# A recurrence on TensorE: four filling products between weighted values and turned scores are taken out, three put in front of state steps, one behind the turns

## The reference, cut to what matters

```python
def rwkv7_mixer(p, mu, w0, w2, a0, a2, g2, k_k, k_a, r_k, lnx_w, lnx_b):
    ...
    def step(S, inp):
        r_t, k_t, v_t, w_t, kk_t, a_t = inp
        sa = jnp.einsum('bhvk,bhk->bhv', S, -kk_t)
        S = (S * w_t[:, :, None, :]
             + sa[..., None] * (kk_t * a_t)[:, :, None, :]
             + v_t[..., None] * k_t[:, :, None, :])
        y = jnp.einsum('bhvk,bhk->bhv', S, r_t)
        return S, y

def first_block(...):
    hn = rms_norm(h, norm_mix_pre[l])
    p = hn @ w_in[l]
    p_rw, p_ret, g_rw, g_ret = _split(p, IN_SIZES)
    y_rw = rwkv7_mixer(p_rw, ...)
```

## Time and profile before

| | |
|---|---|
| median of three executions | 2320.08 us |
| the profiled execution's own time | 2319.33 us |
| its span, first to last instruction | 2317.5 us |
| granted TensorE clock, mean | 0.999 |
| TensorE busy | 2281.6 us (98%), 12764 matmuls |
| VectorE / ScalarE / GpSimd busy | 1380.8 / 752.1 / 914.4 us |
| chain that ended last | TensorE 88%, VectorE 6%, ScalarE 2% |

### The profile page before, as it was taken

The page is one execution under the profiler, slowest core; times in us unless marked ns, Lnnn a source line. Parts: engine busy times, 40 slices in busy tenths (PEclk is TensorE's granted clock), DMA queues, the critical chain, the costliest instruction groups (busy, mean ns, idle before and its releaser), DMA issues.

```text
span 2317.5 us, 33458 instructions
## 1 busy us (share of the span) xinstructions
PE 2281.6 (98%) x12764; PEld 1882.9 (81%) x12764; DVE 1380.8 (60%) x1615; ACT 752.1 (32%) x1243; POOL 914.4 (39%) x538
## 2 busy tenths in 40 slices
PE   7999999999999999999999999999999999999998
PEld 6788888888888888888888887888888887777776
DVE  7755374537543754576628796555551487756775
ACT  4311131113111211334325334444432445114442
POOL 3311231123112313413366457777744445422164
PEclk9999999999999999999999999999999999999999
DMA  3211211121111113573544432222156433211123
GB/s 148 81 55 46 74 55 55 55 72 47 64 55 65 64 46 115 196 236 133 191 140 146 165 107 82 82 82 82 64 198 210 145 122 100 67 59 40 34 82 119
DMA packets 71317, 230.65 MB, mean 100 GB/s; under 512 B 6800, under 2 KB 11024, under 8 KB 70672
## 3 DMA queue, kind: packets, MB, share of 16 engines
q1 hardware_dynamic: 40560, 138.76, 18.8%
q10 hardware_dynamic: 30624, 89.97, 10.6%
HBM read 182.04 MB, written 46.66 MB: 99 GB/s over the span
## 4 chain that ended last, share of the span: by engine, by line
PE 88%; DVE 6%; ACT 2%; issue 1%; DVEq 1%; POOL 1%; DMA 1%; POOLq 0%; ACTq 0%; SPq 0%
PE psg L774 7%; PE psg L779 7%; PE psg L781 6%; PE psg L640 4%; PE psg L645 4%; PE psg L644 4%; PE psa L1246 3%; PE psa L1248 2%; PE psa L1249 2%; PE psb L1246 2%; PE psb L1248 2%; PE psb L1249 2%; PE psa L874 2%; PE psb L861 1%; PE psg L742 1%; PE psg L1458 1%
## 5 line engine op out<-in xcount | busy, mean ns | idle before, releaser
L527 POOL CAST whi<-wraw 128x1024 fp32r<-128x1024 f32 (+1 forms) x144 | 167.0, 1159 | 1102.4 <-PE psg L774 512.0
L529 POOL TENSOR_TENSOR wlo<-wraw,whi 128x1024 fp32r<-128x1024 f32 (+1 forms) x144 | 367.8, 2554 | 20.8 <-issue 0.2
L774 PE MATMUL psg<-xhi,whi 128*128 128x512 f32 x640 | 259.2, 405 | 0.0
L781 PE MATMUL psg<-xhi,wlo 128*128 128x512 f32 x640 | 258.0, 403 | 0.0
L779 PE MATMUL psg<-xlo,whi 128*128 128x512 f32 x640 | 256.2, 400 | 0.0
L640 PE MATMUL psg<-xhi,whi 128*128 128x512 f32 x496 | 195.7, 394 | 2.7 <-issue 2.1
L645 PE MATMUL psg<-xhi,wlo 128*128 128x512 f32 x496 | 194.8, 393 | 0.0
L644 PE MATMUL psg<-xlo,whi 128*128 128x512 f32 x496 | 193.9, 391 | 0.0
L604 POOL TENSOR_TENSOR wlo<-wraw,whi 128x1024 fp32r<-128x1024 f32 (+1 forms) x50 | 112.1, 2243 | 139.8 <-ACT whi L2783 74.3
L774 PEld LDWEIGHTS psg<-xhi,whi 128*128 128x128 f32 x640 | 120.9, 189 | 25.8 <-issue 6.3
L781 PEld LDWEIGHTS psg<-xhi,wlo 128*128 128x128 f32 x640 | 120.8, 189 | 20.9 <-issue 1.0
(11 more groups left out here) (699 smaller groups left out, 5873.9 us busy)
## 6 DMA issues: line engine op xcount, KB each, us to landing
wraw<-w SPq DMA_DIRECT2D x208, 512.0 KB, 3.5
later_scratch<-stage ACTq DMA_DIRECT2D x40, 512.0 KB, 2.6
sraw<-w SPq DMA_DIRECT2D x16, 512.0 KB, 3.9
ff_scratch<-ring ACTq DMA_DIRECT2D x10, 512.0 KB, 2.6
ff_scratch<-ff ACTq DMA_DIRECT2D x10, 512.0 KB, 2.6
ff<-ff_scratch ACTq DMA_DIRECT2D x5, 1024.0 KB, 7.6
RV<-later_scratch SPq DMA_DIRECT2D x4, 1024.0 KB, 11.9
RG<-later_scratch SPq DMA_DIRECT2D x4, 1024.0 KB, 5.6
```

The lines of the kernel that those rows point to most:

```text
L527: pool.tensor_copy(whi[:, u, 0:width], wraw[:, u, 0:width])
L529: pool.tensor_tensor(wlo[:, u, 0:width], wraw[:, u, 0:width], whi[:, u, 0:width].bitcast(F32), ALU.subtract).then_inc(w_ready, 1)
L774: mm = pe.matmul(ps[:, cols], whi[:, slot, w_cols], xhi[:, k, cols], start=(k == 0), stop=False)
L781: mm = pe.matmul(ps[:, cols], wlo[:, slot, w_cols], xhi[:, k, cols], start=False, stop=(k == KT - 1))
```

## The change

In each of the 16 groups, the four fillings between L842 and L849 go. The fillings behind L849 become six instead of five. Three single fillings are put in: behind outputs(1) and so in front of step(0,1), behind additions(1,0) in front of step(1,0), behind additions(1,1) in front of step(1,1). The sum over a group stays 87.

```diff
                     mm.then_inc(sem("dv_full"), 1)
-                    fill(4)
 
                     pe.wait_ge(sem("at_unit"), 4 * i + g + 1)
                     for q in range(4):
                         mm = pe.transpose(bank[2][:, q * P:q * P + P], SC[:, q, 0:P], m(M_ID))
                     mm.then_inc(sem("x_full"), 1)
-                    fill(5)
+                    fill(6)
...
                     state_step(0, 0)
                     outputs(1)
+                    fill(1)
                     state_step(0, 1)
                     additions(1, 0)
+                    fill(1)
                     state_step(1, 0)
                     additions(1, 1)
+                    fill(1)
                     state_step(1, 1)
                 fill(16)
```

## The result

The changed kernel takes 2332.24 us (median of six executions, 2331.0 to 2332.74) against 2319.31 us for the kernel before in the same comparison: ratio 1.0055, 95% interval 1.0045 to 1.0065, or 12.9 us more. It was forecast to be slower, at 2329.9 us within 2324.0 to 2333.5, so direction and range hold. The sum gave 9.8 us more than before, 3 us too few.

The account below looks back on a forecast made before the run. TensorE, busy 98% of the span, was taken as the bound. Sixteen groups at -0.92 + 0.23 + 1.28 = +0.59 give +9.4, with 0.4 for M +9.8 us: forecast 2329.9 us, range 2324 to 2333.5.

Parts of the forecast that it names:

- Removed fillings: Four fillings between L842 and the turned scores L849 go: gain 0.92 us a group.
- The sixth filling: One more filling behind the turned scores L849, same shape on both sides: adds 0.23 us a group.
- Three fillings in the state part: Each makes two array-shape changes of one: 0.42 for each of two, 0.44 for the third, 1.28 us a group.
- A group +0.59: Sum for one group: -0.92 + 0.23 + 1.28 us; sixteen groups +9.4 us.
- this reading: The 0.15 us gap before L933 is the price of changing the array part in use, not a wait.
- M late in a pair's second group: L861's weight load waits for VectorE's M: 0.1 us in four of sixteen groups, 0.4 us in all.
- What else the moved fillings carry: Products end in the same gaps or one later; shifted signals to VectorE, GpSimd and SyncE cost nothing.
- The third rival: VectorE becomes the bound before L861 in all groups: 0.25 us in sixteen, 2333.5 us, up to 2340; chance 0.08.
- the forecast's narrower case: The forecast case for the whole kernel, 2327.5 to 2332.5 us, given 0.80.
- Weights loaded ahead: First rival: state-part fillings' weights load during narrow products, each adds 0.31 us; 2324.3 us in all; chance 0.06.
- A filling hidden in the wait for the copy: Second rival: the gap before L933 is the wait for ScalarE's copy; 2315.8 us, wholly hidden 2309.0; chance 0.06.

Follow-up runs that it names:

- the kernel with one shape: steps_unwaited with both products of a state step using all 128 rows, so the state part is 128*64 throughout; ratio 0.9942 to the kernel before.
- steps_unwaited: The kernel before, with L933 and L941 reading PT instead of the state and not waiting for ScalarE's copy; ratio 1.0 to the kernel before.
- the split one: The changed kernel with GpSimd's subtraction L529 made as two subtractions of half the columns; 2340.97 us, ratio 1.0092 to the kernel before.

## Why the prediction was right, and where it fell short

**Right, to a few hundredths.** Removed fillings 0.92: measured 0.97 (1.81 to 0.84). The sixth filling 0.23: 1.84 instead of 1.60. Three fillings in the state part 0.42, 0.42 and 0.44: each 0.44 or 0.45. A group +0.59: +0.58. The sum worked because both ways of a filling, in and out, had rows with the same shapes elsewhere in the trace, and because a gap next to a wait was checked against the same gap without one. The kernel without the wait and the kernel with one shape show that this reading holds. The Trainium skill, TensorEngine Tiling (Array Packing), Key Properties, says that changing the tiling mode drains TensorE; by that rule the gap goes when the shape stays, and the trace agrees (0.15 to 0.00). It is not the whole account: in front of the narrow fp32r filling the gap stayed at 0.20 though the shape did not change.

**Right as a mechanism, small.** M late in a pair's second group: taken at 0.1 us, four times. DVE and then PEld of the changed kernel, in the second group:

```profile
380.70 0.69 DVE L1755 TENSOR_TENSOR rw_M<-psb,mat 128x512 fp32r<-128x512 f32 x1
```

```profile
381.45 0.52 PEld L860 LDWEIGHTS psb<-rw_M,rw_ATH 128*128 128x128 f32 x4 [0.27 <-DVE rw_M L1755]
```

M ends at 381.39 and releases the weight load at 381.45, which had to wait for it; all that follows in the level comes 0.11 later than in the other groups.

**The step that failed** is in "What else the moved fillings carry": "Products end in the same gaps of TensorE's work as before otherwise, or one gap later, with levels to spare", and "these edits I cost at nothing: their cover is VectorE's and GpSimd's idle time". One gap later was right, but the end of a product matters for more than the one who takes its result. It starts GpSimd, and while GpSimd's L529 runs, VectorE's operations on two SBUF tiles do not end. In the second group the cover was gone for ATL, and the group lost 0.6 us at L889 and L890, not at L861 or L774, where I had said that a lateness would show: 2.4 us that were missing from the sum. The third rival named "the fillings' new timing puts GpSimd's work over it", but placed it in front of L861 and in all groups. I had rows that show the block: MT takes 0.89 and 1.15 in a pair's first two groups and 0.69 in the other two. In the first it ends 0.54 after L529, in the second (at 375.38) 0.55 after GpSimd's copy L527 (at 374.83), in the kernel before:

```profile
373.79 1.04 POOL L527 CAST whi<-wraw 128x1024 fp32r<-128x1024 f32 x1 [19.69 <-PE psg L774]
```

I priced only that operation with it; the right step was to list every VectorE operation on two SBUF tiles and lay GpSimd's new times over them. The Trainium skill, SBUF — State Buffer, Who interferes with whom, says that a VectorE instruction with two SBUF inputs contends with a GpSimd instruction that reads SBUF, and calls such contention an exclusive lock. The traces agree: VectorE ends 0.55 after L529 in the two kernels and 0.55 after the first half in the split one.

That 2332.24 still lies in the forecast's narrower case (2327.5 to 2332.5) is in part luck: nothing in that case stood for these 2.4 us. The upper figure of the third rival is also mis-added: 0.25 us and fillings at 0.65 in all sixteen groups come to 2344, not 2340; no term of the sum hangs on it.

**The rivals.** Weights loaded ahead (adds 0.31): refuted by 0.43. A filling hidden in the wait for the copy: refuted by steps_unwaited.

**Open.** The type in the way into a narrow filling, as said above. Whether a state part in one shape can be had with its right values: it would need PT and RT with zeros in the other head's rows, and the copy's wait, now hidden, may then bind (the copy ends at 366.58, the last L921 starts at 366.60). This was not tried. Of the versions here that compute the same values, none beats the kernel before beyond the interval.

## What to carry to other kernels

A busy engine's gap next to a wait need not be that wait: look for the same pair of lines where nothing is waited for, before something is put into the gap. Fill in at places where the array's shape stays as it is, and better also the type, and if it must be elsewhere, in one place and not in three (0.43 for the first, 0.23 for the next). When work that signals other engines is moved, lay the times of what it sets off over the operations that it can hold up, even where its result is needed much later.

## What the runs showed of the hardware that was not expected

- Between products of one narrow shape (128*64), an fp32r product behind fp32 ones stood 0.20 us behind the last of them, its weight load with it; a pair of fp32 ones stood 0.09 behind, its weights loaded ahead. Between full 128*128 lines, L842 in fp32 and the fp32r fillings, no such gap shows: four fillings cost 0.97 together.
- VectorE's subtraction of two SBUF tiles, 0.68 us alone, took 1.43, 2.57 or 1.46 us, each time ending about 0.55 us after GpSimd's running subtraction or its first half; operations that read PSUM and one SBUF tile (M, 0.69) were not lengthened under the same GpSimd work.
- It goes both ways: GpSimd's subtraction, 2.40 us alone, took 2.65 where it began during VectorE's MT, and its two halves took 4.50 in place of 2.54 where VectorE's L1701 ran between them.
- GpSimd's subtraction of 1024 columns took 2.40 us in one instruction and about 2.54 us in two of 512.
- Behind 2.4 us in which TensorE started nothing (311.69 to 314.05) and 1.0 us of fillings 0.23 apart, its granted clock was 0.50 in 315.10 to 318.50; the kernel's mean is 0.996.
